# A three-block transformer kernel: the second block's tail in two sections without inner barriers, and the delta scan's output products in another order

## The chip, the cores and the metric

One core of one Trainium2 chip runs the whole program. The metric is the device time of one execution in microseconds (us). Engines are named as in the profile: PE is TensorE's matmul, PEld its weight loads, DVE VectorE, ACT ScalarE, POOL GpSimd, SP SyncE, which issues the DMAs.

## The reference, cut to what matters

Three blocks work on x, 512 tokens of 1024 features, all in float32. What the change touches is the end of the second block, the head of the third, and one recurrence:

```
att_x = blocked_mla(...) @ w_o_mla                      # 8 heads x 128
y_conv = silu(layer_norm(u, ln_g, ln_b)) @ w_pw         # u: depthwise convolution's result
x = x + mx[2] * ((sigmoid(g_conv) * y_conv + sigmoid(g_mla) * att_x) @ w_out)
h = modulate(rms_norm(x, g_ffn), mx[3], mx[4])
a, b = split(h @ w_13);  x = x + mx[5] * ((silu(a) * b) @ w_2)      # hidden width 2816
x = rms_norm(x, g_final)                                # end of the second block
h = layer_norm(x, ln_in_g, ln_in_b)                     # third block
pool_in = h @ w_in[:, :512]                             # then windowed means of pool_in
# gated delta rule, 8 chunks of 64 tokens, 8 heads, state 128 x 128 per head:
v_new = u_n - w_n @ state
o     = qg_n @ state + attn_n @ v_new
state = state * exp(gl_n) + kg_n.T @ v_new
```

## The kernel before, in words

**Layout.** Activations lie feature-major: x is 8 tiles of 128 features by 512 tokens. Every weight matrix comes as a stream of chunks of 512 KB, each 8 tiles of 128 x 128. SP loads chunks into a ring of three (`raw`, `load_chunk` L138). ACT rounds a chunk to the float32r part `whi` (`make_hi`, L144), DVE subtracts to get the rest `wlo` (`make_lo`, L149); both rings have three slots. An activation is split in the same way into `hi` and `lo`, and a product is three matmuls: hi by wlo, lo by whi, hi by whi (L233 to L235 in `linear`, L171 to L173 in `products`). A chunk is therefore 24 matmuls of 128 x 512. A slot is refilled only when the PE is done with its chunk: `next_hi` (L159) waits for `chunk_done`, `next_lo` (L164) follows it, `next_load` (L153) follows that.

**Stages.** `stage` (L73) opens a block of engine programs that ends with a barrier of all engines and a clearing of semaphores. `dense` (L239) is one stage: eight or more output tiles over the stream, evacuated from four PSUM banks. `split_tiles` (L466) is a stage that makes hi and lo of eight tiles. `norm` (L349) is a stage too: with `center` first the sum over features as a product with a matrix of ones (L367), the mean (L378), the subtraction (L399); then squares (L384) and their sum (L371), the factor as Ln and Exp (L386, L388), the scaling (L417), the shift (L421) and, where the output is split, L391 and L406. In the second block after the attention come, each as a stage or two of this kind: split of the attention's output and `dense` by w_o; `norm` of the convolution's result, SiLU with a reload of x, split and `dense` by w_pw; split and `dense` by w_out, which adds into x (L2387); `ffn` (L482): `norm`, `swiglu` (L429, 44 chunks), `dense` over 22 tiles in 24 chunks, `added` (L2396); `norm` by g_final. `third_block` (L2971) goes on with `norm`, and `pool_branch` (L2464) with a memset stage, `dense` of four chunks (L343), the window sums (L2490 to L2500), a split and the product by pool_w.

**The other style.** `macro` (L90) is a block as well, but several matrix products follow in it one after another: each engine has one hand-written program with its own waits. The first block, `conv_and_gates` (L1828) and the attention are written so. `Feed`, `Factor`, `Copies` and `Shift` are pieces of such programs: a `lead` runs two chunks tile by tile, as the activation's tiles come.

**The delta scan** (`delta_scan`, L2751) runs 8 steps. Per step PE makes the state's products (L2779), the solve (L2785), the state's update (L2791) and then, for each of 8 heads, one product with the state's 128 x 128 weights (L2798) and one with 64 x 128 weights (L2799) that adds to the same 64 columns. Each of them is a plain float32 matmul, which the profile shows as two passes. Between the groups lie slices of a background product (three and two per step, three matmuls each). L2835 adds to the state on DVE, L2812 decays it on POOL, L2844 copies the output on ACT.

Of the kernel before, what the change touches and what calls it, by code (L numbers as in the profile page):

```python
# [6 lines left out]
F32 = mybir.dt.float32  # L7
F32R = mybir.dt.float32r
# [538 lines left out]
class Factor:  # L547


    def __init__(self, k, m, x, sq, tmp, rs, bank):  # L550
        self.k, self.x, self.sq, self.tmp, self.rs, self.bank = k, x, sq, tmp, rs, bank
# [8 lines left out]
    act_factor, pe_square = Feed.act_factor, Feed.pe_square  # L560


class Copies:
# [1772 lines left out]
def second_block(k, x, rs, modx, modc, gains, ctx_d, rope_d):  # L2336
# [25 lines left out]
    with nc.sbuf_tensor("gates_place", [P, 72 * 256 + 64], F32):  # L2362
        with nc.sbuf_tensor("o_hi", [P, DT, SEQ], F32R) as oh, \
                nc.sbuf_tensor("o_lo", [P, DT, SEQ], F32R) as ol:
            split_tiles(k, qn, (oh, ol), 8)
            dense(k, DT, DT, (oh, ol), nothing, scaled_by(k, gates[:, 8:16, :], gates[:, 8:16, :]))
        with nc.sbuf_tensor("conv_hi", [P, DT, SEQ], F32R) as uh, \
                nc.sbuf_tensor("conv_lo", [P, DT, SEQ], F32R) as ul:
            mid = u[:, :, HALO:HALO + SEQ]
            norm(k, mid, DT, SEQ, D, 1e-6, lambda t: col(k, "ln_g", t), mid,  # L2370
                 shift=lambda t: col(k, "ln_b", t), center=True)
            with stage(nc, "silu_ready", "landed_x") as (block, silu_ready, landed):
                @block.sync
                def _(sp):
                    sp.dma_start(x[:, :, :], x_saved).then_inc(landed, 16)
                    sp.wait_ge(landed, 16)

                @block.scalar
                def _(act):
                    act.activation(mid, mid, ACT.Silu).then_inc(silu_ready, 1)  # L2380
            split_tiles(k, mid, (uh, ul), 8)
            dense(k, DT, DT, (uh, ul), nothing,
                  scaled_by(k, gates[:, 0:8, :], gates[:, 0:8, :], gates[:, 8:16, :]), ("scaled",))
            split_tiles(k, gates, (uh, ul), 8)

            def add_gated(dve, f, half, bank, S):
                dve.scalar_tensor_tensor(tile_at(x, f), k.ps[:, bank, :], modx[:, bass.ds(f + 16, 1)],  # L2387
                                         tile_at(x, f), ALU.mult, ALU.add).then_inc(S.acc_free, 1)
            dense(k, DT, DT, (uh, ul), nothing, add_gated)

    def add_ffn(y):
        with stage(nc, "added") as (block, added):
            @block.vector
            def _(dve):
                for t in range(DT):
                    dve.scalar_tensor_tensor(x[:, t, :], y[:, t, :], modx[:, 40 + t:41 + t], x[:, t, :],  # L2396
                                             ALU.mult, ALU.add).then_inc(added, 1)
    ffn(k, x, lambda h: norm(k, x, DT, SEQ, D, 1e-6, gf, h, shift=lambda t: modx[:, 24 + t:25 + t]),
        add_ffn)
    norm(k, x, DT, SEQ, D, 1e-6, lambda t: col(k, "g_final", t), x)  # L2400

def norm_tiles(k, tiles, gain, scale, eps, ones="ones", bg=Idle(), slices=0, place=None):
# [55 lines left out]
                    bg.dve(dve, gaps[n // 4])  # L2461


def pool_branch(k, h, mix):  # L2464

    nc = k.nc
    pad = 16
    with ExitStack() as ctx:
        sb = lambda n, s, d=F32: ctx.enter_context(nc.sbuf_tensor(k.name(n), s, d))
        u = sb("pool_in", [P, 4, pad + SEQ])  # L2470
        s = sb("pool_sum", [P, 2, pad + SEQ])
        d = sb("pool_diff", [P, 4, SEQ])
        dh, dl = sb("pool_hi", [P, 4, SEQ], F32R), sb("pool_lo", [P, 4, SEQ], F32R)
        with stage(nc, "zeroed") as (block, zeroed):
            @block.gpsimd
            def _(gp):
                gp.memset(u[:, :, 0:pad], 0.0).then_inc(zeroed, 1)
                gp.memset(s[:, :, 0:pad], 0.0).then_inc(zeroed, 1)
        dense(k, 4, DT, h, copy_out(k, u[:, :, pad:]), nothing)
# [271 lines left out]
def delta_scan(k, q, key, k_tok, v_tok, xt, attn, beta, egc, egl, out, bg, slices):  # L2751
# [3 lines left out]
    with ExitStack() as ctx:  # L2755
# [15 lines left out]
        @block.tensor  # L2771
        def _(pe):
            pe.wait_ge(zeroed, 1)
            for j in range(8):
                tp, T, tk, S = rows(j), j // 2, slice(64 * j, 64 * j + 64), s2[:, j % 2, :, :]
                if j:
                    pe.wait_ge(s_ready, j)
                for h in range(8):
                    mm = pe.matmul(k.ps[tp, h // 4, (h % 4) * P:(h % 4 + 1) * P], key[:, h, tk], S[:, h, :],  # L2779
                                   start=True, stop=True)  # L2780
                mm.then_inc(ks_ready, 1)
                bg.pe(pe, gaps[3 * j])
                pe.wait_ge(r0_ready, j + 1)
                for h in range(8):
                    mm = pe.matmul(k.ps[tp, h // 4, (h % 4) * P:(h % 4 + 1) * P], xt[tp, h, T, :],  # L2785
                                   r0[tp, h, :], start=True, stop=True)
                mm.then_inc(u_done, 1)
                bg.pe(pe, gaps[3 * j + 1])
                pe.wait_ge(vn_ready, j + 1)
                for h in range(8):  # L2790
                    mm = pe.matmul(k.ps[:, 2 + h // 4, (h % 4) * P:(h % 4 + 1) * P],  # L2791
                                   k_tok[tp, T, h * P:(h + 1) * P], vn[tp, h, :], start=True, stop=True)
                mm.then_inc(s_done, 1)
                if j >= 2:
                    pe.wait_ge(o_kept, j - 1)
                for h in range(8):
# [171 lines left out]
        dense(k, n, DT, h, act_evac, dve_evac, ("relu_ready", "sq_ready", "hi_done"))  # L2968


def third_block(k, x, p_d):  # L2971
    nc = k.nc
    gain = lambda name: (lambda t: col(k, name, t))
    with ExitStack() as outer:
        h = tuple(outer.enter_context(nc.sbuf_tensor(n, [P, DT, SEQ], F32R)) for n in ("h3_hi", "h3_lo"))
        norm(k, x, DT, SEQ, D, 1e-5, gain("ln_in_g"), h, shift=gain("ln_in_b"), center=True)
        pool_branch(k, h, x)
# [51 lines left out]
def bass_three_blocks(nc, wstream, vecs, mats, x_t, lora, g_up, c_rows, wmod, ctx_t, rope_t, p_t, out):  # L3029
# [8 lines left out]
    with ExitStack() as ctx:  # L3038
# [18 lines left out]
        second_block(k, x, rs, modx, modc, gains, ctx_t, rope_t)  # L3057
        third_block(k, x, p_t)
        with stage(nc, "stored") as (block, stored):
            @block.sync  # L3060
            def _(sp):
# [193 lines left out]
```

## Time and profile before

| | |
|---|---|
| median of 3 runs | 3924.54 us (3923.83 to 3925.13) |
| profiled execution | 3924.69 us, its span 3922.9 us |
| busy share: PE, DVE, ACT, POOL | 88 %, 45 %, 30 %, 4 % |
| mean granted TensorE clock | 0.912 of full |
| DMA queues' packets | 22.1 % of 16 engines' span |

The span is the time from the first to the last instruction. A group's mean is the duration of one instruction; matmuls overlap, so a matmul's pace is the distance of two starts, which is shorter than its duration. The granted clock is 1.0 at 2.4 GHz and 0.5 at 1.2 GHz.

### The profile page before, as it was taken

What the parts mean: (1) busy time and instruction counts of PE and PEld (TensorE: products, weight loads), DVE (VectorE), ACT (ScalarE), POOL (GpSimd) and SP (SyncE); (2) the same over time, 40 slices, a digit from 0 to 9 for tenths busy, and PEclk for the clock granted to TensorE, in tenths of its full rate; (3) what the DMA queues carried; (4) which work ended last, traced back from release to release, by engine and by line L of the source; (5) the groups of instructions that cost most, each with busy time, mean ns of one, the idle gap of its engine ahead of it and who ended that gap; (6) DMA issues with size and microseconds to landing.
All of it is one profiled execution on the core that took longest, in us unless ns stands there. A gap on an engine that the chain in (4) does not pass through costs nothing. (4 is left out here: it accounts for less than half of the span.)

```text
span 3922.9 us, 43448 instructions
## 1 busy us (share of the span) xinstructions
PE 3434.3 (88%) x17830; PEld 2637.6 (67%) x17830; DVE 1772.0 (45%) x2698; ACT 1191.8 (30%) x1714; POOL 145.0 (4%) x174
## 2 busy tenths in 40 slices
PE   8999988987999999999867999769877896799986
PEld 6887766774688778744555887447656684577764
DVE  4447555533544568577343332335523333433323
ACT  3333332215333333333222222323352202231322
POOL 0000001110000000000000000000014300000000
PEclk9999996788999999989988999879979976899998
DMA  3335210001233633200121222112200000122222
GB/s 130 97 126 207 84 58 8 2 7 57 78 97 122 210 105 98 77 22 0 44 75 59 95 94 93 58 43 89 99 12 23 23 17 32 49 86 89 89 82 74
DMA packets 75221, 285.25 MB, mean 73 GB/s; under 512 B 8336, under 2 KB 8464, under 8 KB 73872
## 3 DMA queue, kind: packets, MB, share of 16 engines
q1 hardware_dynamic: 75024, 282.47, 22.1%
q8 instruction: 142, 2.33, 0.2%
q14 instruction: 55, 0.45, 0.0%
HBM read 276.15 MB, written 6.29 MB: 72 GB/s over the span
## 5 line engine op out<-in xcount | busy, mean ns | idle before, releaser
L149 DVE TENSOR_TENSOR wlo<-raw,whi 128x1024 fp32r<-128x1024 f32 x450 | 552.2, 1227 | 1367.6 <-ACT whi L144 1367.4
L144 ACT ACTIVATE whi<-raw 128x1024 fp32r<-128x1024 f32 x450 | 476.3, 1059 | 1440.4 <-PE ps L235 869.2
L233 PE MATMUL ps<-h_hi,wlo 128*128 128x512 f32 x968 | 389.3, 402 | 94.5 <-DVEq L204 94.5
L234 PE MATMUL ps<-h_lo,whi 128*128 128x512 f32 x968 | 387.6, 400 | 0.0
L235 PE MATMUL ps<-h_hi,whi 128*128 128x512 f32 x968 | 387.1, 400 | 0.0
L171 PE MATMUL ps<-h_hi,wlo 128*128 128x512 f32 x832 | 341.3, 410 | 40.8 <-PEq L80 21.2
L172 PE MATMUL ps<-h_lo,whi 128*128 128x512 f32 x832 | 328.4, 395 | 0.0
L173 PE MATMUL ps<-h_hi,whi 128*128 128x512 f32 x832 | 328.2, 394 | 0.0
L233 PEld LDWEIGHTS ps<-h_hi,wlo 128*128 128x128 f32 x968 | 185.1, 191 | 144.4 <-issue 99.0
L171 PEld LDWEIGHTS ps<-h_hi,wlo 128*128 128x128 f32 x832 | 158.4, 190 | 88.6 <-issue 41.0
L235 PEld LDWEIGHTS ps<-h_hi,whi 128*128 128x128 f32 x968 | 185.0, 191 | 45.7
L234 PEld LDWEIGHTS ps<-h_lo,whi 128*128 128x128 f32 x968 | 185.3, 191 | 45.2
L233 PE MATMUL ps<-mid_hi,wlo 128*128 128x512 f32 x432 | 173.3, 401 | 12.5 <-DVEq L204 12.5
L173 PEld LDWEIGHTS ps<-h_hi,whi 128*128 128x128 f32 x832 | 158.7, 191 | 34.6
L172 PEld LDWEIGHTS ps<-h_lo,whi 128*128 128x128 f32 x832 | 159.1, 191 | 31.9 <-issue 2.2
L1787 DVE SCALAR_TENSOR_TENSOR conv_acc<-u,vecs,conv_acc 128x512 f32<-128x512 f32 x232 | 173.9, 750 | 5.8
L234 PE MATMUL ps<-mid_lo,whi 128*128 128x512 f32 x432 | 172.6, 400 | 0.0
L235 PE MATMUL ps<-mid_hi,whi 128*128 128x512 f32 x432 | 172.6, 400 | 0.0
L173 PE MATMUL ps<-mid_hi,whi 128*128 128x512 f32 x352 | 136.9, 389 | 0.0
L171 PE MATMUL ps<-mid_hi,wlo 128*128 128x512 f32 x352 | 136.9, 389 | 0.0
L172 PE MATMUL ps<-mid_lo,whi 128*128 128x512 f32 x352 | 136.9, 389 | 0.0
L171 PE MATMUL ps<-hx_hi,wlo 128*128 128x512 f32 x304 | 121.9, 401 | 11.1 <-PEq L104 6.5
(545 smaller groups left out, 5846.8 us busy)
## 6 DMA issues: line engine op xcount, KB each, us to landing
raw<-in_wstream SPq DMA_DIRECT2D x453, 512.0 KB, 3.5
mod_ring<-in_wmod SPq DMA_DIRECT2D x48, 512.0 KB, 4.5
c_rows<-in_c_rows SPq DMA_DIRECT2D x3, 1024.0 KB, 5.6
x<-in_x_t SPq DMA_DIRECT2D x4, 512.0 KB, 8.6
x_saved<-x SPq DMA_DIRECT2D x1, 2048.0 KB, 8.9
x<-x_saved SPq DMA_DIRECT2D x1, 2048.0 KB, 7.7
mix_saved_d<-x SPq DMA_DIRECT2D x1, 2048.0 KB, 8.6
mix_back<-mix_saved_d SPq DMA_DIRECT2D x1, 2048.0 KB, 7.8
```

The lines of the kernel that those rows point to most:

```text
L144: act.activation(k.whi[:, n % SPLIT, :], k.raw[:, n % RAW, :], ACT.Copy).then_inc(k.hi_ready, 1)
L149: dve.tensor_tensor(k.wlo[:, n % SPLIT, :], k.raw[:, n % RAW, :], k.whi[:, n % SPLIT, :].bitcast(F32), ALU.subtract).then_inc(k.split_read ...
L171: pe.matmul(out, wlo, hi, start=first, stop=False)
L172: pe.matmul(out, whi, lo, start=False, stop=False)
L173: return pe.matmul(out, whi, hi, start=False, stop=last)
L233: pe.matmul(out, lo, xhi, start=first, stop=False)
L234: pe.matmul(out, hi, xlo, start=False, stop=False)
L235: mm = pe.matmul(out, hi, xhi, start=False, stop=last)
L1787: dve.scalar_tensor_tensor(out, row[:, tap:tap + SEQ], w, acc[:, :], ALU.mult, ALU.add)\
```

## The change

1. From the attention's end to the third block's pooling input there are two `macro` sections: `merge_branches` (24 chunks) and `gated_feed_forward` (44 + 24 + 4 chunks). `pool_branch` keeps its memset stage (now of one tile) and loses its `dense`.
2. In `merge_branches` the convolution's layer norm is done between the chunks of the w_o product, its first sum as seven additions on DVE and one product. In `gated_feed_forward` the silu product's high part is copied by ACT instead of cast by DVE (L449); squares for the two factors go between the chunks; normed values go straight to hi and lo (`Shift`), without L421.
3. `delta_scan` issues the eight products with the state, then the eight with v_new.

The diff, cut; "..." stands for what is left out.

```diff
+def merge_branches(k, x, u, gates, modx, rs, x_saved):
...
+        def _(sp):
+            for i in range(24):
+                next_load(k, sp, g0 + i)
+                if i == 0:
+                    sp.wait_ge(copies.lo, DT)
+                    sp.dma_start(x[:, :, :], x_saved).then_inc(x_in, 16)
...
+            lead(0, copies.lo, oh)
+            for i in range(2, 8):
+                chunk(i, oh)
+                if i == 2:
+                    pe.wait_ge(summed, DT - 1)
+                    pe.matmul(k.ps[:, 4, :], mat(k, "ones"), total[:, :], start=True, stop=True).then_inc(mean_done, 1)
+                if i in (3, 4):
+                    for t in range(4 * (i - 3), 4 * (i - 2)):
+                        conv_square(t)
+            lead(8, lo, ch)
+            for i in range(10, 16):
+                chunk(i, ch)
+            lead(16, g_lo, gh)
+            for i in range(18, 24):
+                chunk(i, gh)
+                factor.pe_square(pe, i - 18)
+            factor.pe_square(pe, 6)
+            factor.pe_square(pe, 7)
...
+            for i in range(24):
+                next_hi(k, act, g0 + i)
...
+                if i == 4:
+                    act.preload_act_table_set("natural_log_exp_and_others")
...
+                    act.preload_act_table_set("silu_and_others")
+                if i in (4, 5):
+                    for t in range(4 * (i - 4), 4 * (i - 3)):
+                        conv_tile(t)      # Silu into mid[t], then Copy into ch[0]
...
+            factor.act_factor(act)
+            act.preload_act_table_set("silu_and_others")
...
+def gated_feed_forward(k, x, modx, gain, rs, pool_in):
...
+            lead(g0, feed)
+            for i in range(2, 2 * FFT):
...
+            for f in range(DT):
+                for c in range(3):
...
+                    if f == 0:
+                        pe.wait_ge(mid_lo, kts[-1] + 1)
...
+                if f:
+                    factor.pe_square(pe, f - 1)
+            factor.pe_square(pe, DT - 1)
+            for t in range(DT):
+                pe.wait_ge(normed, t + 1)
+                mm = pe.matmul(k.ps[:, 6, :], mat(k, "ones"), x[:, t, :], start=t == 0, stop=t == DT - 1)
+            mm.then_inc(mean_done, 1)
+            for t in range(DT):
+                factor3.pe_square(pe, t)
+            lead(gp0, feed3)
+            for i in range(2, 4):
...
@@ delta_scan
                 for h in range(8):
-                    o = k.ps[:, 4 + j % 2, h * 64:h * 64 + 64]
-                    pe.matmul(o, S[:, h, :], q[:, h, tk], start=True, stop=False)
-                    mm = pe.matmul(o, vn[tp, h, :], attn[tp, h, T, :], start=False, stop=True)
+                    pe.matmul(o(h), S[:, h, :], q[:, h, tk], start=h == 0, stop=False, skip_group_check=True)
+                for h in range(8):
+                    mm = pe.matmul(o(h), vn[tp, h, :], attn[tp, h, T, :], start=False, stop=h == 7,
+                                   skip_group_check=True)
```

## Rows read from the trace of the kernel before

**Rows 1.** Stretches from the attention's last matmul to pool_w's first: us, then busy us (count)

```profile
core 0: us, PE busy (x) PEld busy (x) DVE busy (x) ACT busy (x) POOL busy (x), PEclk, DMA share, GB/s
1884.40:1891.40 7.00, 0.05 (x2) 0.07 (x1) 4.90 (x8) 4.87 (x9) 0.00 (x0) 0.77 0.01 1
1891.40:1938.10 46.70, 46.68 (x192) 37.04 (x192) 12.76 (x14) 7.41 (x7) 0.00 (x0) 0.96 0.26 79
1938.10:1983.50 45.40, 14.63 (x32) 5.42 (x33) 20.91 (x34) 17.17 (x22) 0.00 (x0) 0.78 0.16 58
...
2030.20:2040.20 10.00, 0.04 (x1) 0.00 (x0) 7.42 (x11) 5.32 (x9) 0.00 (x0) 0.74 0.18 52
...
2087.60:2120.20 32.60, 9.81 (x16) 3.48 (x17) 16.59 (x26) 14.90 (x21) 0.00 (x0) 0.69 0.05 16
2120.20:2368.50 248.30, 248.26 (x1056) 198.60 (x1056) 88.78 (x106) 57.62 (x66) 0.00 (x0) 0.99 0.29 91
...
2373.10:2498.00 124.90, 124.86 (x528) 100.29 (x528) 28.19 (x23) 27.84 (x30) 0.00 (x0) 0.99 0.30 95
2498.00:2564.30 66.30, 26.60 (x49) 9.71 (x49) 31.61 (x49) 24.88 (x35) 0.21 (x2) 0.72 0.04 15
...
2588.40:2606.70 18.30, 0.00 (x1) 0.00 (x1) 14.39 (x27) 3.73 (x6) 0.00 (x0) 0.58 0.09 30
sum 722.30, PE 589.00 PEld 448.41 DVE 262.96 ACT 184.28 POOL 0.21; mean PE 45.31 PEld 34.49 DVE 20.23 ACT 14.18 POOL 0.02
```

**Rows 2.** Waits of PE in 1884 to 2607: us, times, longest

```profile
PE ps L233 <- DVEq L204: 103.9, 7, 25.5
```

**Rows 3.** Groups of instructions in 1884 to 2607

```profile
L149 DVE TENSOR_TENSOR wlo<-raw,whi 128x1024 fp32r<-128x1024 f32 x96 | 117.7, 1226 | 380.8 <-ACT whi L144 380.8
L144 ACT ACTIVATE whi<-raw 128x1024 fp32r<-128x1024 f32 x96 | 101.7, 1060 | 438.0 <-PE ps L235 438.0
L384 ACT ACTIVATE sq<-x 128x512 f32<-128x512 f32 x24 | 14.9, 628 | 21.2 <-PE ps L371 11.0 <-PEq L80 9.5 <-DVE x L399 0.8
L2387 DVE SCALAR_TENSOR_TENSOR x<-ps,modx,x 128x512 f32<-128x512 f32 x8 | 6.0, 745 | 0.0
L399 DVE TENSOR_TENSOR u<-u,rstd 128x512 f32<-128x512 f32 x8 | 4.9, 684 | 8.1 <-ACT rstd L378 8.1
L388 ACT ACT_TABLE_LOAD x3 | 3.8, 1283 | 0.1
```

**Rows 4.** A stretch at full clock, and the eight steps of the delta scan

```profile
2140.00:2340.00 200.00, 200.00 (x859) 160.29 (x858) 75.04 (x90) 45.78 (x53) 0.00 (x0) 1.00 0.29 95
3120.70:3281.40 160.70, 158.49 (x760) 130.58 (x760) 48.21 (x42) 11.91 (x17) 15.18 (x8) 0.75 0.06 19
```

**Rows 5.** Timeline: sums of squares in the norm before pooling

```profile
2537.18 7.52 PE L371 MATMUL ps<-sq,mats 128*128 128x512 f32 x16 [2.08 <-ACT sq L384]
```

**Rows 6.** Timeline: how `conv_and_gates`, written as a macro section, begins

```profile
1386.43 0.63 ACT L519 ACTIVATE rs<-acc 128x512 f32<-128x512 f32 x1
...
1387.38 1.41 DVE L1811 SCALAR_TENSOR_TENSOR val<-x,mod_gains,rs 128x512 f32<-128x512 f32 x2 [3.37 <-PEq L104]
...
1390.27 0.76 PE L171 MATMUL ps<-hx_hi,wlo 128*128 128x512 f32 x1 [4.60 <-DVE hx_lo L1820]
```

**Rows 7.** Timeline: the third step of the delta scan, update, outputs, next step's first products

```profile
3171.36 2.05 PE L2791 MATMUL ps<-r,k_tok 64*128 64x128 f32 x16
3173.34 0.43 PE L2798 MATMUL ps<-qkv,state 128*128 128x64 f32 x2
...
3173.71 0.43 PE L2799 MATMUL ps<-attn,r 64*128 64x64 f32 x2
...
3181.36 0.69 PE L2799 MATMUL ps<-attn,r 64*128 64x64 f32 x2
3181.97 3.57 PE L2779 MATMUL ps<-state,qkv 128*64 128x128 f32 x16
```

**Rows 8.** Timeline: products of one kind in a row, in the first block's scan and in `delta_matrices`

```profile
861.73 1.10 PE L1410 MATMUL ps<-rw,state 128*128 128x64 f32 x8
...
2919.14 1.95 PE L2710 MATMUL ps<-qkv 128*128 128x128 f32 x16
```

More of the change, by code:

```diff
@@ L547, with __init__ @@
 class Factor:
-    def __init__(self, k, m, x, sq, tmp, rs, bank):
-        self.k, self.x, self.sq, self.tmp, self.rs, self.bank = k, x, sq, tmp, rs, bank
+    def __init__(self, k, m, x, sq, tmp, rs, bank, eps=1e-6):
+        self.k, self.x, self.sq, self.tmp, self.rs, self.bank, self.eps = k, x, sq, tmp, rs, bank, eps
         self.sq_ready, self.sq_used = m.sem("factor_sq_ready"), m.sem("factor_sq_used")
@@ L558, in act_tile, with act_factor @@
         act.activation(self.sq[:, t % 2, :], self.x[:, t, :], ACT.Square).then_inc(self.sq_ready, 1)
-    act_factor, pe_square = Feed.act_factor, Feed.pe_square
+    def act_factor(self, act):
+        act.wait_ge(self.sq_used, DT)
+        act.activation(self.tmp, self.k.ps[:, self.bank, :], ACT.Ln, bias=self.k.eps[self.eps], scale=1.0 / D)\
+           .then_inc(self.logged, 1)
+        act.wait_ge(self.logged, 1)
+        act.activation(self.rs, self.tmp, ACT.Exp, scale=-0.5).then_inc(self.rs_ready, 1)
+    pe_square = Feed.pe_square
 class Copies:
@@ L2360, in second_block @@
         mla_attention(k, qn, qr, kn, kr, vt, scratch, at(k, "mla_stats", 140, [P, 2, 8]), u, acc)
[L2362 to L2394, printed above, removed]
-                for t in range(DT):
[L2396 to L2400, printed above, removed]
+    factor_rs = at(k, "ffn_factor", 136, [P, SEQ])
@@ L2461, in _, with pool_branch @@
                     bg.dve(dve, gaps[n // 4])
-def pool_branch(k, h, mix):
+def pool_branch(k, h, mix, u):
     nc = k.nc
@@ L2469, in pool_branch @@
         sb = lambda n, s, d=F32: ctx.enter_context(nc.sbuf_tensor(k.name(n), s, d))
-        u = sb("pool_in", [P, 4, pad + SEQ])
         s = sb("pool_sum", [P, 2, pad + SEQ])
@@ L2476, in _ @@
             def _(gp):
-                gp.memset(u[:, :, 0:pad], 0.0).then_inc(zeroed, 1)
                 gp.memset(s[:, :, 0:pad], 0.0).then_inc(zeroed, 1)
-        dense(k, 4, DT, h, copy_out(k, u[:, :, pad:]), nothing)
         with stage(nc, "step", "hi_ready", "lo_ready") as (block, step, hi_ready, lo_ready):
@@ L2795, in _ @@
                     pe.wait_ge(o_kept, j - 1)
+                o = lambda h: k.ps[:, 4 + j % 2, h * 64:h * 64 + 64]
                 for h in range(8):
-                    o = k.ps[:, 4 + j % 2, h * 64:h * 64 + 64]
-                    pe.matmul(o, S[:, h, :], q[:, h, tk], start=True, stop=False)
-                    mm = pe.matmul(o, vn[tp, h, :], attn[tp, h, T, :], start=False, stop=True)
+                    pe.matmul(o(h), S[:, h, :], q[:, h, tk], start=h == 0, stop=False, skip_group_check=True)
+                for h in range(8):
+                    mm = pe.matmul(o(h), vn[tp, h, :], attn[tp, h, T, :], start=False, stop=h == 7,
+                                   skip_group_check=True)
                 mm.then_inc(o_done, 1)
@@ L2968, in relu_square, with third_block @@
         dense(k, n, DT, h, act_evac, dve_evac, ("relu_ready", "sq_ready", "hi_done"))
-def third_block(k, x, p_d):
+def third_block(k, x, h, pool_in, p_d):
     nc = k.nc
@@ L2974, in third_block @@
     with ExitStack() as outer:
-        h = tuple(outer.enter_context(nc.sbuf_tensor(n, [P, DT, SEQ], F32R)) for n in ("h3_hi", "h3_lo"))
-        norm(k, x, DT, SEQ, D, 1e-5, gain("ln_in_g"), h, shift=gain("ln_in_b"), center=True)
-        pool_branch(k, h, x)
+        outer.enter_context(nc.sbuf_tensor("h3_place", [P, 32 * 256 + 64], F32))
+        with nc.sbuf_tensor("pool_place", [P, 9 * 256], F32):
+            pool_branch(k, h, x, pool_in)
         with nc.sbuf_tensor("qkv3", [P, 24, SEQ], F32) as qkv:
@@ L3056, in bass_three_blocks @@
         rs, modx, modc, gains = first_block(k, x, vecs, mats, x_t, lora, g_up)
-        second_block(k, x, rs, modx, modc, gains, ctx_t, rope_t)
-        third_block(k, x, p_t)
+        h, pool_in = second_block(k, x, rs, modx, modc, gains, ctx_t, rope_t)
+        third_block(k, x, h, pool_in, p_t)
         with stage(nc, "stored") as (block, stored):
```

279 lines of the change are left out of this document (added).

## The prediction

> **What bounds the kernel now.** I read the busy shares first: PE at 88 % of the span, so time is PE's work, its pace, and its gaps. Then I cut the changed stretch, from the attention's last matmul to the first product by pool_w, into its stages [rows 1]. It lasts 722.3 us with PE busy for 589.0. The stages are of two kinds. In the dense ones PE never stops: 192 matmuls take 46.7 us, the 44 chunks of the gated product 248.3. Between them PE idles or does a few sums: 7.0, 45.4, 10.0, 32.6, 66.3 and 18.3 us, and 4.6 more between 2368.5 and 2373.1. The waits of PE say the same: 103.9 us in seven waits at the start of a dense stage [rows 2], where PE stands at a barrier while DVE and ACT prepare a whole activation. The pace at full clock is 200/859 = 0.233 us a matmul [rows 4], 5.6 us a chunk; a dense stage of eight chunks should take 44.8 and takes 46.7, since its first matmuls run at 1.2 GHz (clock 0.96) after the gap. So each gap costs itself and about 1.9 us.
>
> ACT and DVE have room: in the gated product DVE is busy 88.8 of 248.3 us, ACT 57.6, DMA 29 % [rows 1].
>
> The delta scan is another picture: 160.7 us for eight steps, PE busy nearly throughout, granted clock 0.75 [rows 4]. Of a step of 20.1 us the output products take 3181.97 - 3173.34 = 8.63 us for 32 passes [rows 7].
>
> **The change, part by part.** Sections first, as seen by PE.
>
> *Opening.* Eight tiles are split before a barrier now: 7.0 us [rows 1]. With a lead, one tile suffices: seven ACT copies of 0.62 (one pass, as L384 [rows 3]) and the closing barrier (some 0.4) go, 2.3 us are left.
>
> *First section, stream.* 24 chunks are 134.4 us; one ramp stays, 1.8: 136.2. Added among them are single float32 sums. Eight of them took 7.52 us [rows 5], 0.94 each with some waiting; I take 0.9 in a stream. The section has 17 (1 for the mean, 8 convolution squares, 8 of x), down from 24 in the two norms; 14 lie between chunks: 12.6 us.
>
> *First section, the one new wait.* The convolution's SiLU and copies stand on ACT behind the refills of chunks 7 and 8, four tiles each time. A tile costs ACT two passes, 2 x 0.63, and DVE 0.75 + 0.69 [rows 3], in a chain of about 1.4 us. I followed the queues: chunk 4 ends, ACT refills (1.06), loads a table (1.28), waits for the last square, takes Ln and Exp and a second table load, then four tiles, 5.6 us. By then chunk 5 is over; refill 8, four more tiles, and only then refill 9, whose DVE half (1.23) ends about 3 us after chunk 7. The lead of w_pw needs chunk 9, so PE waits **3.1 us**, between 0 (if DVE and ACT overlap better) and 12 (if the two chains run one after another). Squares and subtractions before it are ready when PE comes to them.
>
> *The other two leads.* At chunk 15's end ACT and DVE need 1.06 + 1.23 + 3 x 0.69 + 0.62 = about 5 us for the last merged tile, but the lead uses that tile 9.8 us later: no gap, where 10.0 us and a ramp were.
>
> *First section's tail.* After chunk 23: refill 2.3, the sum into x 0.75, square 0.63, waits: 4.0; last sum 0.9; Ln and Exp 1.4; table load 1.28; barrier 0.3; then values, high and low part of the first tile. The existing section gives 1390.27 - 1387.38 = 2.9 us for the last step, with a table load of ACT in it [rows 6]; here it lies ahead of the barrier, so 2.3. Sum 10.2.
>
> First section: 2.3 + 136.2 + 12.6 + 3.1 + 10.2 = 164.4, against 7.0 + 46.7 + 45.4 + 46.7 + 10.0 + 47.4 + 32.6 = 235.8 us (the two dense stages not shown are of the pattern of the first). **Saved 71.4.**
>
> *Second section.* The gated product keeps 248.3; its lead is paced by DVE (2 x 0.75 a tile against PE's 1.4), +0.3. The cast leaves DVE for ACT, both under cover: per two chunks ACT has 2 x 1.06 + 2 x 0.62 = 3.4 us in 11.2. The 4.6 us gap goes. The product over 22 tiles is 22 x 5.6 = 123.2, plus six sums of 0.9: 128.6 (124.9 before, with a ramp). Then the two norms, 66.3 us now. After: last tile's sum to factor 6.3, eight scalings 6.0 with the feature sums behind them (PE lags at the low clock, +2.7), mean 0.7, subtraction and first square 1.4, eight sums 7.5 [rows 5], factor 1.5, first tile of the lead 2.4: 28.5. The two sums are chained by data, so the change can't remove them; four table loads of 1.28, three barriers, L2396's 6 us and seven tiles of splitting go. Pool's four chunks: 24.3 (24.1 before). After them 18.3 us, now with one more stage in the way (the memset): +1.3. Sum 248.6 + 128.6 + 28.5 + 24.3 + 19.6 = 449.6 against 486.5. **Saved 36.9.**
>
> Costed at nothing: x's reload (2 MB) now stands in SP's queue between weight loads. A ring of three raw chunks covers 16.8 us, and DMA is at 30 % at most [rows 1]; without that cover the next refill would be late by the reload's time. POOL's memset in the second section is waited for by nobody but the end. Together **108.3**, bounds 98 (the wait at 12, one more ramp) and 118 (no wait, no lag).
>
> *Delta scan.* Alternating, two passes are 0.37 us apart at full clock and 0.61 at the low one (3173.71 - 3173.34, 3181.97 - 3181.36) [rows 7]. Products of one kind in a row: eight passes of exactly this shape, 128 x 128 weights and 64 columns, in 1.10 us including the last one's run-out, and 16 with 128 columns in 1.95 [rows 8]: 0.115 a pass. Low clock: 3.57/16 = 0.22 (L2779) [rows 7]. The clock falls inside the group, where PE streams little: 10 passes at 0.185 and 22 at 0.305 make the 8.6 us, so some 2 us in. Over the scan it is at the low level half of the time (0.75). Three outcomes per step:
> - clock stays up: outputs 32 x 0.115 = 3.7, next products 1.9 instead of 3.57, the rest 7.9: 13.5, saving 6.6, **52** in all;
> - clock drops 2 us in as now: 17 passes done by then, 15 more at 0.22, next products at 3.57: 5.3 + 3.57 + 7.9 = 16.8, saving 3.3, **27**;
> - pace is not set by the alternation: **0**.
>
> Grouped passes still stream 64 columns per load of 128, so PE stays half empty there; I take the middle. DVE's addition to the state, 1.2 us for 1024 columns as L149's [rows 3], is ready before the outputs' 3.7 us are over, and POOL's decay (15.18/8 = 1.9 us [rows 4]) is wanted only after the next update; neither becomes late.
>
> Here the row and a rule differ. Rows 8 show weights of the same shape loading beside the running matmul: 16 passes at 0.12 us, where a load of 128 x 128 alone is busy for 37.04/192 = 0.19 [rows 1]. The Trainium skill (TensorE: Matmul & The Clock Gate, "The mechanism") says that weight loads overlap with running matmuls only when the row group differs; with that, grouping like with like gains nothing. The trace speaks against it, and it is the third outcome above. The same page ("What's actually happening") holds that activity releases the throttle; the first outcome would be that rule at work.
>
> **Sum.** The profiled execution is 3924.7 us (span 3922.9 and 1.8 around it), 0.1 above the median. 3924.7 - 108.3 - 27 = **3789**.
>
> **Rivals.**
> - *Clock stays up in the scan.* For: denser passes. Against: they are still half empty. 3924.7 - 108.3 - 52 = 3764.
> - *The order in the scan buys nothing.* Against it rows 8, for it that only the alternating pair was ever seen with accumulation. 3816.
> - *The first section stalls.* The layer norm's chain is 12 us late and later gaps pull the clock down, also in the second section's tail: some 20 us back, 3809.
> - *Slower than before.* The mechanism: in a barrier-free section refills stand behind other work on ACT's and DVE's queues; once the way from a chunk's end to its slot's refill (2.3 us bare) exceeds the two chunks in hand, 11.2 us, PE waits at every chunk. To lose 8 us net each of the 96 chunks would have to wait (135 + 8)/96 = 1.5 us. Against it: DVE's busiest chunk in the steady part has 3.3 us, only chunks 4 and 5 have more. 3933.
>
> **How the numbers follow.** Forecast 0.59, clock up 0.15, order nothing 0.12, first section stalls 0.11, slower 0.03. The range takes the forecast with its bounds and most of the next two: 3760 to 3816. Within 0.2 % (8 us, what a measurement can tell) lies almost nothing: 0.01; faster 0.96.
>
> **What would show it.** Right: no wait of PE over 4 us between attention and pooling except before the second section (10 us) and in the two norms (28); one of about 3 at w_pw's lead; the stretch to pool_w's first product 614 us long; in the scan 5.3 us from the first output product to the next step's first, steps of 16.8. Wrong: output passes further apart than 0.13 us at full clock, a granted clock in the scan still at 0.75, or PE waiting for `wlo` inside a chunk stream.

## The result, and the profile of the changed kernel

The changed kernel takes **3747.36 us** (median of 4 runs, 3744.08 to 3754.97) against 3924.18 (4 runs beside it, 3919.36 to 3925.13): ratio 0.9554, 95 % interval 0.9541 to 0.9568. I had forecast 3789, and 3760 to 3816 as the range. The sign was right, the size was 42 us short. The profiled execution is 3744.08 us, its span 3742.1.

The stretches of the changed kernel, to be laid beside [rows 1] and [rows 4]; columns as there:

```profile
1876.38:1929.56 53.18, 53.18 (x210) 40.48 (x210) 34.24 (x49) 27.78 (x40) 0.00 (x0) 0.97 0.27 99
...
1932.65:2036.11 103.46, 96.02 (x401) 76.05 (x401) 44.68 (x55) 31.78 (x38) 0.00 (x0) 0.96 0.29 92
2036.11:2402.00 365.89, 365.89 (x1592) 300.73 (x1593) 122.34 (x131) 105.60 (x125) 0.00 (x0) 0.99 0.31 95
2402.00:2436.44 34.44, 23.41 (x43) 8.78 (x41) 14.50 (x22) 11.31 (x17) 0.15 (x1) 0.80 0.10 31
2436.44:2460.09 23.65, 23.64 (x96) 19.05 (x96) 12.23 (x16) 8.87 (x12) 0.00 (x0) 0.93 0.22 67
...
2990.75:3105.10 114.35, 111.61 (x760) 96.36 (x760) 48.30 (x42) 11.90 (x17) 15.18 (x8) 0.97 0.08 27
2100.00:2280.00 180.00, 180.00 (x796) 149.07 (x795) 60.69 (x67) 53.30 (x66) 0.00 (x0) 1.00 0.32 97
```

The first section (1873.96 to 2036.11, with the two waits of 2.4 and 3.1 us that the next view shows) takes 162.2 us, the second with the stage behind it 443.0. Together 605.1, against 722.3 before. The waits of PE in this stretch (us in all, times, longest). Before, the seven waits at the start of a dense stage took 103.9 us [rows 2], and those in the norms 29.5 more:

```profile
PE ps L233 <- DVEq L204: 19.0, 1, 19.0
PE ps L171 <- DVE h_lo L1827: 9.3, 2, 5.4
PE ps L528 <- ACT sq L558: 4.9, 2, 2.9
PE ps L171 <- DVE wlo L149: 3.1, 1, 3.1
PE ps L171 <- DVE o_lo L582: 2.4, 1, 2.4
PE ps L2632 <- DVE x L2713: 2.2, 1, 2.2
PE ps L528 <- ACT conv_sq L558: 2.0, 1, 2.0
```

Of the seven waits at the start of a dense stage one is left, the 19.0 us ahead of pool_w. A step of the scan, which answers to [rows 7]:

```profile
3028.57 2.05 PE L3114 MATMUL ps<-r,k_tok 64*128 64x128 f32 x16
3030.55 2.00 PE L3123 MATMUL ps<-qkv,state 128*128 128x64 f32 x16
3032.48 2.00 PE L3125 MATMUL ps<-attn,r 64*128 64x64 f32 x16
...
3034.40 1.96 PE L3102 MATMUL ps<-state,qkv 128*64 128x128 f32 x16
```

From the first output product to the next step's first product are 3.85 us; before 8.63. The scan takes 114.35 us instead of 160.7, at a granted clock of 0.97 instead of 0.75.

**Where the 180.8 us of the two profiled spans come from**, read off the times of the same landmarks in both:

| part | before | after | difference | forecast |
|---|---|---|---|---|
| up to the attention's end (code unchanged) | 1884.4 | 1874.0 | -10.4 | 0 |
| attention's end to pool_w's first product | 722.3 | 605.1 | -117.2 | -108.3 |
| from there to the scan | 514.0 | 511.7 | -2.3 | 0 |
| delta scan | 160.7 | 114.35 | -46.4 | -27 |
| after the scan | 641.5 | 636.9 | -4.6 | 0 |

The first row is not the change's. In both kernels the same program runs there, and its time differs from one execution to the next: it has more than one course. The changed kernel from 590 to 640 us, columns as above (the granted clock stands third from the end), first in the profiled execution, then in a later one of the same kernel (a13 below):

```profile
590.00:640.00 50.00, 41.22 (x618) 33.41 (x618) 30.61 (x116) 16.18 (x53) 9.91 (x14) 0.89 0.01 2
```

```profile
590.00:640.00 50.00, 44.18 (x392) 35.39 (x392) 22.35 (x94) 12.57 (x42) 8.49 (x12) 0.62 0.03 12
```

At 0.62 the attention ends at 1885.6, as in the kernel before (1884.4). Of the 18 traces of this study two end it by 1875.4, two between 1878.7 and 1880, thirteen between 1883 and 1886, and one (a3), whose first block has its operands moved, at 1914. What tips it I did not find. The totals below carry this difference, so runs are compared by stage. Ten of the fifteen variants were timed once; their totals rest on one execution each.

### The profile page after: what moved, and what is told of

Its sections match the earlier page's. It is cut to its first block and busy times, and to the rows that moved or that the text cites. A ratio compares the mean times of both kernels' runs of the same rounds, so it can differ in the third digit from the quotient of the medians.

```text
span 3742.1 us, 43214 instructions
## 1 busy us (share of the span) xinstructions
PE 3339.5 (89%) x17816; PEld 2592.6 (69%) x17816; DVE 1754.9 (47%) x2659; ACT 1201.4 (32%) x1732; POOL 145.0 (4%) x174
## 3 DMA queue, kind: packets, MB, share of 16 engines
q1 hardware_dynamic: 75024, 282.47, 23.3%
## 5 line engine op out<-in xcount | busy, mean ns | idle before, releaser
L171 PE MATMUL ps<-mid_hi,wlo 128*128 128x512 f32 x528 | 207.8, 394 | 0.0
L173 PE MATMUL ps<-mid_hi,whi 128*128 128x512 f32 x528 | 205.4, 389 | 0.0
L172 PE MATMUL ps<-mid_lo,whi 128*128 128x512 f32 x528 | 205.4, 389 | 0.0
L172 PE MATMUL ps<-hx_lo,whi 128*128 128x512 f32 x304 | 120.0, 395 | 0.0
L173 PE MATMUL ps<-hx_hi,whi 128*128 128x512 f32 x304 | 119.6, 393 | 0.0
L171 PEld LDWEIGHTS ps<-mid_hi,wlo 128*128 128x128 f32 x528 | 99.1, 188 | 21.9 <-issue 1.4
```

Of the source, the lines that this page charges most:

```text
L171: pe.matmul(out, wlo, hi, start=first, stop=False)
L172: pe.matmul(out, whi, lo, start=False, stop=False)
L173: return pe.matmul(out, whi, hi, start=False, stop=last)
```

## Experiments: the delta scan's order

**One part alone, from both sides.** a1 puts the old order into the changed kernel, b1 the new order into the old one.

```diff
+                for h in range(8):
+                    pe.matmul(o, S[:, h, :], q[:, h, tk], start=True, stop=False)
+                    mm = pe.matmul(o, vn[tp, h, :], attn[tp, h, T, :], start=False, stop=True)
```

> The changed kernel with the delta scan's outputs in the old, alternating order. Nothing else is touched. Theory (the scan's 46 us come from the order alone, as pace and as clock): the scan goes from 114 us back to about 160, granted clock in it from 0.97 to about 0.75, the time from 3747 to 3793. Rival (the scan gained because the stages ahead of it now leave the clock in a better state, the order gives only part): the scan stays between 125 and 145 us, time 3760 to 3778.

> The kernel before with the new order in the delta scan and nothing else. Theory (order alone): scan 160.7 to about 114 us, time 3924 - 46 = 3878. My forecast's own case (the clock still drops): 3924 - 27 = 3897, granted clock about 0.85. Rule that like row groups cannot overlap their loads: 3924.

Measured: a1 3803.1 us (ratio to before 0.969, interval 0.9668 to 0.9711; the 10 us over the expected 3793 are the first block's longer course, its attention ends at 1885.1), b1 3880.8 (0.9892, interval 0.9868 to 0.9915). The scans, a1 then b1:

```profile
3004.00:3163.40 159.40, 157.71 (x760) 130.13 (x760) 48.20 (x42) 11.90 (x17) 15.15 (x8) 0.76 0.06 19
```

```profile
3122.50:3238.80 116.30, 113.75 (x760) 98.03 (x760) 48.29 (x42) 11.90 (x17) 15.16 (x8) 0.95 0.08 26
```

The order alone is worth 45.1 and 44.4 us in the scan, whatever stands ahead of it. Both rivals fall, my forecast's 27 among them.

**What in the order costs.** Two things had changed at once: how often the kind of weights changes, and whether a product adds to the 64 columns just written. a4 keeps the first and takes away the second; a5 does the reverse, with the state's product made twice per head, and so leaves out the product of attn and v_new. Both orders in short form:

```diff
# a4                                       # a5
+for h in range(9):                        +for h in range(8):
+    if h < 8: state(h)                    +    state(h)
+    if h: values(h - 1)                   +    state(h)     # adds to the same columns
```

> The changed kernel, outputs in the order state(0), state(1), values(0), state(2), values(1) and so on: kinds alternate, but the two products of one head no longer follow each other on the same 64 columns of PSUM. Theory A (a switch between weights of 128 rows and weights of 64 rows costs): passes 0.185 us apart at full clock, outputs 8.6 us, clock falls as in the kernel before, scan 160 us. Theory B (adding to the columns just written costs): 0.12 us a pass, outputs 3.9 us, scan 114 us.

> The changed kernel; per head the product with the state is made twice, one right behind the other, the second adding to the columns of the first. It leaves out the product of attn and v_new in the outputs. Theory A (switch of shapes costs): no switches, 0.12 us a pass, outputs 3.9 us, scan 114 us. Theory B (adding to columns just written costs): about 0.185 us a pass and 160 us.

Timelines of PE, a4 and then a5:

```profile
3054.77 0.43 PE L3123 MATMUL ps<-attn,r 64*128 64x64 f32 x2
3055.13 0.43 PE L3122 MATMUL ps<-qkv,state 128*128 128x64 f32 x2
3055.49 0.43 PE L3123 MATMUL ps<-attn,r 64*128 64x64 f32 x2
```

```profile
3025.78 3.79 PE L3122 MATMUL ps<-qkv,state 128*128 128x64 f32 x32
3029.49 1.96 PE L3102 MATMUL ps<-state,qkv 128*64 128x128 f32 x16
```

a4: still 0.36 us for a pair of passes, scan 156.8 us, 3799.9 in all. a5: 32 passes in 3.71 us, scan 111.8. So it is the change between products of 128 rows and products of 64, not the accumulation. Weights and moving operand change their rows together; no run parts the two. The traces show where the time goes: in a row of one kind the load of the next weights begins 0.055 us after the start of the pass before it (changed kernel), and at a change 0.20 us after it (a1, at 3037.04 behind 3036.83). The Trainium skill (TensorE: Matmul & The Clock Gate, "The mechanism") has loads overlap with running matmuls only where the row group differs. The traces do not bear that out: in a row of one kind a load onto the same rows begins 0.055 us into a pass that lasts 0.275, and the order in which the rows change is the slower one. a6 halves the number of changes:

```diff
+for h in range(0, 8, 2):
+    state(h); state(h + 1); values(h); values(h + 1)
```

> The changed kernel, outputs in groups of two heads: two state products, two value products, and so on (8 changes of kind per step where the old order has 16 and the new one 2). If each change of kind costs PE 2 x (0.185 - 0.12) = 0.13 us at full clock: 3.9 + 6 x 0.13 = 4.7 us for the outputs as long as the clock holds. If the clock holds the scan is 114 + 8 x 0.8 = 121 us; if it falls as in the old order, outputs 7 and next products 3.5 us, scan about 150.

```profile
3045.86 0.66 PE L3122 MATMUL ps<-qkv,state 128*128 128x64 f32 x4
...
3050.56 3.24 PE L3102 MATMUL ps<-state,qkv 128*64 128x128 f32 x16
```

Outputs 3050.56 - 3045.86 = 4.70 us at full clock, just as priced at 0.13 us a change. The scan takes 143.1 us at a clock of 0.80 (3780.9 in all): between the two, and nearer the slow one. In this step the clock fell 5.2 us behind the first output, when the outputs were over; in the other seven it fell 2.0 to 3.7 us behind it, among them.

**The clock.** At full clock throughout, the alternating outputs would take 32 x 0.1825 = 5.84 us, 2.0 more than the grouped ones. That is 16 us in eight steps; by this estimate the other 30 of the 46 are the clock, which in the old order is low for the later outputs and the next step's products. Two runs ask what holds it up: a7 adds two large products among alternating outputs, a10 makes the grouped outputs twice over.

```diff
# a7, in the old order's loop over h
+    if h in (2, 5):
+        pe.matmul(k.ps[:, 0, :], mat(k, "ident"), q[:, h, :], start=True, stop=True)
# a10
+for again in range(2):
+    for h in range(8): state(h)
+    for h in range(8): values(h)
```

> The changed kernel with the old, alternating order and two extra float32 products of 512 columns per step among the outputs (behind heads 2 and 5, into a bank that is free there, result unused). Theory (the alternation's small products leave PE too idle, so the clock falls, and that is two thirds of the 46 us): with dense work between them the clock stays up; outputs 32 x 0.185 + 2 x 0.9 = 7.7 us, next products 1.95, steps about 17.6, scan some 141 us although work was added. Rival (the clock isn't what slows the outputs): 160 + 8 x 1.8 = 175 us.

> The changed kernel, new order, every step's output products made twice over (8 state, 8 value, and the same again, which writes the same result). Added: 16 products, 32 passes a step. If the density of the passes keeps the clock up: 8 x 3.85 = 31 us more, scan 145 us at a granted clock of 0.97, time 3778. If the length of the stretch of small products decides, whatever their order: the clock falls in the second half, outputs about 10 us and next products 3.5, scan about 114 + 8 x 8 = 178 us, granted clock about 0.8.

```profile
3032.70 0.62 PE L3122 MATMUL ps<-qkv,state 128*128 128x64 f32 x2
3033.25 0.69 PE L3123 MATMUL ps<-attn,r 64*128 64x64 f32 x2
3033.87 2.07 PE L3125 MATMUL ps<-qkv,mats 128*128 128x512 f32 x2
...
3127.57 1.13 PE L3125 MATMUL ps<-qkv,mats 128*128 128x512 f32 x2
```

```profile
3037.05 2.00 PE L3122 MATMUL ps<-qkv,state 128*128 128x64 f32 x16
...
3040.91 2.00 PE L3122 MATMUL ps<-qkv,state 128*128 128x64 f32 x16
3042.84 3.37 PE L3123 MATMUL ps<-attn,r 64*128 64x64 f32 x16
3046.13 3.67 PE L3102 MATMUL ps<-state,qkv 128*64 128x128 f32 x16
...
3123.67 2.38 PE L3123 MATMUL ps<-attn,r 64*128 64x64 f32 x16
```

My theory fell in a7 by its number: 178.3 us for the scan, where the rival had 175 and I 141. In the step shown the clock had fallen before the first added product, and two of them did not bring it back; the first four steps went like it, with the clock falling 1.6 to 2.0 us behind the first output. In the fifth and the seventh it fell 0.2 and 0.4 us after the first added product had begun. In the sixth (3127.57) and the eighth both added products went at full pace (1.13 us for 2.07) and the clock stayed up through the outputs: the sixth step took 19.2 us where the first five took 23.3 to 24.5.

In a10 the scan takes 175.6 us where 178 stood for "the length of the stretch decides", and the clock falls in each of the eight steps, in grouped order too. In the step shown first, passes go at 0.12 us until some 6 us behind the first output. That is the latest of the eight: the others fall 3.4 to 5.9 us behind it, and in two of them within the first sixteen products (3123.67). In the alternating order the clock falls in every step as well, 1.9 to 3.6 us behind the first output (a1; 1.5 to 3.3 in the kernel before). With grouped outputs made once it falls in one of the changed kernel's eight steps, 4.2 us behind the first output and among the next products (L3102 3.41 us at 3048.25), and in one of b1's, 2.9 us behind it; in a5 it falls in none.

So that grouping holds the clock up is shown, from both sides. Why is not shown in full. With the length doubled at the same density it was lost in every step (a10), which speaks for the length; but in two of these steps it fell before the second half began, so what went before in the scan plays a part too. Grouped outputs are also denser than alternating ones, and no run changed the density alone. The time of the fall moves by up to 3 us from step to step within one trace, and that it would fall in only one step of eight could not be worked out from these figures. The Trainium skill (TensorE: Matmul & The Clock Gate, "What's actually happening") says that activity releases the throttle; a7's sixth step agrees, and its first steps show that added activity behind the fall was not enough here.

## Experiments: where the operands lie

In the changed kernel at full clock 796 products go in 180 us, 0.226 each; before, 859 in 200, 0.233 [rows 4]. The difference follows the moving operand. Before, activations of the dense stages start 64 bytes past a multiple of 128 (h3_hi at byte 79168 of its partition in the built program); hand-placed ones start at a multiple (79232). The sections use hand-placed ones, and so does h3, which the third block reads. Four runs move operands and nothing else.

```diff
# b2, a2 (16 floats), b3 (8 floats)      # a3
+        sb("pad", [P, 16])              -        k.arena = PERSISTENT
         k.arena = PERSISTENT            +        k.arena = PERSISTENT - 64
```

> The kernel before with one unused tensor of 64 bytes a partition ahead of the stack's later tensors, so that every activation of the dense stages starts 64 bytes later: at a multiple of 128 bytes, where it was 64 past one. Nothing else changes. Theory (the moving operand's start sets the pace): all 128x512 products of the dense stages go from 0.2333 to 0.2267 us apart, some 5200 of them, 5200 x 0.0066 = 34 us, time 3924 to 3890. Rival (the pace belongs to the style of the stage: loops, semaphores, bank order): no change, 3924.

> The changed kernel with the same 64-byte tensor. Only the third block's o, mid and p operands (about 1010 products) still start 64 past a multiple of 128 in it. Theory (start of the moving operand): 1010 x 0.0066 = 6.7 us, time 3747 to 3741. Rival (style of the stage): 3747.

> The changed kernel with every hand-placed tensor 64 bytes lower, so that the operands of the barrier-free sections of all three blocks start 64 past a multiple of 128 bytes. Theory (the moving operand's start sets the pace): some 9400 products go from 0.2267 to 0.2333 us; where PE sets the pace that is up to 62 us, time some 3747 + 50 to 60 = 3800 to 3809. Rival (style of the stage): 3747.

> The kernel before with the dense stages' operands 32 bytes higher, 96 past a multiple of 128 bytes (before: 64 past; with 64 bytes more, at the multiple: 0.2267 us a product). If only a start at a multiple of 128 is fast: 0.2333 us, time 3924. If the pace grows with what is off a multiple of 64 too: above 0.2333.

200 us at full clock in b2, b3 and a3; the number behind PE's busy time is its count:

```profile
2140.00:2340.00 200.00, 200.00 (x884) 165.62 (x883) 76.27 (x91) 47.66 (x56) 0.00 (x0) 1.00 0.31 97
```

```profile
2140.00:2340.00 200.00, 200.00 (x859) 161.02 (x858) 75.04 (x90) 46.25 (x54) 0.00 (x0) 1.00 0.30 94
```

```profile
2140.00:2340.00 200.00, 200.00 (x859) 160.29 (x858) 64.92 (x71) 58.07 (x71) 0.00 (x0) 1.00 0.29 95
```

With 64 bytes more the old kernel's stages run at 0.226; with 32 they stay at 0.233; the changed kernel, moved off, falls back to 0.233. The style of the stage has no part in it.

The times are smaller than the counts of products gave. b2: 3905.4 us (ratio 0.9952, interval 0.9936 to 0.9969), 19 us where I expected 34. By stage it gains 10.7 us between attention and pool_w and 10.6 behind the scan, and nothing between them, where it is 2.5 longer (as are b1 and b3 by 2.1 and 2.0, without faster products). In the first of these stretches the dense streams gained 15.3 us, as 96 x 24 x 0.0066 = 15.2 says, and the norm behind w_o gave back 4.6, because its sums ran at the low clock. First the kernel before, then b2:

```profile
1941.35 7.11 PE L367 MATMUL ps<-u,mats 128*128 128x512 f32 x16 [3.27 <-PEq L80]
1950.54 7.52 PE L371 MATMUL ps<-sq,mats 128*128 128x512 f32 x16 [2.07 <-ACT sq L384]
```

```profile
1940.83 10.15 PE L367 MATMUL ps<-u,mats 128*128 128x512 f32 x16 [3.27 <-PEq L80]
1953.06 9.09 PE L371 MATMUL ps<-sq,mats 128*128 128x512 f32 x16 [2.08 <-ACT sq L384]
```

Between pool_w and the scan the q, k, v projection ends with DVE's convolution, so a faster pace there only lengthens PE's wait at the stage's end. This wait is 6.95 us in the kernel before (first row) and 10.67 in the changed kernel (second row), and 10.67 in b2 as well:

```profile
2815.17 0.77 PE L233 MATMUL ps<-h_hi,wlo 128*128 128x512 f32 x1 [6.95 <-DVEq L204]
```

```profile
2685.53 0.77 PE L233 MATMUL ps<-h_hi,wlo 128*128 128x512 f32 x1 [10.67 <-DVEq L204]
```

a2: behind the scan 630.3 us for 636.9, 6.6 where 6.7 was expected. Its median is 3747.8 (ratio 0.9553, interval 0.9532 to 0.9574), since its first block took the longer course (attention's end at 1885.9). a3: 3801.1 us; 11.0 more in the changed stretch (616.1 for 605.1; by the count of products 15.2, but its w_o stream ran at a clock of 1.00 for 0.97 and the tail of the norms was 1.1 us shorter), 2.8 between it and the scan, 3.2 behind the scan, and the attention ends 28.5 us later than in a13 (1914.1 for 1885.6). b3: 3925.1, no change.

## Experiments: the sections

**The first section as stages again** (on operands at the new placement, with one stage more for the factor of x):

```diff
-        merge_branches(k, x, u, gates, modx, factor_rs[:, :], x_saved)
+            split_tiles(...); dense(...); norm(...); stage silu, reload of x
+            split_tiles(...); dense(...); split_tiles(...); dense(..., add_gated)
+        factor_stage(k, x, factor_rs[:, :])
```

> The changed kernel with the first section undone: split, dense, norm, silu, split, dense, split, dense as stages with barriers, as before the change, on operands at the new placement, and one more stage for the factor of x. The second section and the scan's order stay. Theory (the first section's gaps are worth what they last): the stretch from the attention to the gated product goes from 162 to about 235.8 - 3.8 (pace) - 16 (half of the old norm moved into the second section's opening) = 216 us, time 3747 + 54 = 3801. Rival (part of the gain is only moved, since the second section's own stretches lengthen with a denser first section): less than 40 us.

```profile
PE ps L233 <- DVEq L204: 42.3, 3, 25.3
```

The stretch takes 663.2 us for 605.1: the first section is worth 58.1 us there, against 54 expected, and the three waits at barriers are back (6.95, 25.3 and 10.0). The sums of the convolution's norm ran at the low clock, as in b2 (10.11 and 9.09 us, against 7.11 and 7.52 in the kernel before); that is 4.6 us, about what the result lies over 54. The two kernels with this norm behind a w_o stage at the faster pace, b2 and a9, both show it, and those at the slower pace do not; the cause is open. 3813.8 us in all: of the 69.7 us over the changed kernel, 58.1 are these, 1.5 lie in the first block, and 10.3 went behind them (5.4 between pool_w and the scan, 2.0 in it, 2.9 after it), where the code is the same; why, no run shows.

**The wait at w_pw's lead.** Rows of the changed kernel at that lead: ACT comes to its refills behind the last convolution tile, DVE to the first of two behind the last low part.

```profile
1929.76 0.63 ACT L2466 ACTIVATE conv_hi<-u 128x512 fp32r<-128x512 f32 x1
1930.30 1.99 ACT L144 ACTIVATE whi<-raw 128x1024 fp32r<-128x1024 f32 x2
1930.43 0.69 DVE L2511 TENSOR_TENSOR conv_lo<-u,conv_hi 128x512 fp32r<-128x512 f32 x1 [0.59 <-ACT conv_hi L2466]
1931.37 1.23 DVE L149 TENSOR_TENSOR wlo<-raw,whi 128x1024 fp32r<-128x1024 f32 x1 [0.25 <-ACT whi L144]
...
1932.65 0.80 PE L171 MATMUL ps<-conv_hi,wlo 128*128 128x512 f32 x1 [3.10 <-DVE wlo L149]
```

a8 spreads the tiles over three chunks:

```diff
-                if i in (4, 5):
-                    for t in range(4 * (i - 4), 4 * (i - 3)):
+                if i in (4, 5, 6):
+                    for t in range((0, 3, 6)[i - 4], (3, 6, 8)[i - 4]):
```

> The changed kernel with the convolution's tiles on ACT and DVE spread over three chunks (3, 3 and 2 tiles behind the refills of chunks 7, 8 and 9) instead of two (4 and 4). Theory (the lead of w_pw waits because the refill of chunk 9 stands behind eight tiles of other work on both queues): the refill comes some 1.4 us earlier on each queue and the wait of 3.1 us at that lead goes to nearly nothing, about 3 us off the stretch. Rival (the chain through the last tiles sets the lead anyway): the wait stays at about 3 us under another name.

```profile
PE ps L171 <- DVE wlo L149: 0.5, 1, 0.5
```

The wait is gone but for 0.5 us, and with it the low clock behind it: 4.0 us off the first section. Another 3.1 us went in the second section's tail, where the clock was low for 10.2 us instead of 17.1, at a point that this edit only moved in time; that part is luck. The stretch is 598.2 us; the whole, 3749.0, has the first block's longer course (attention's end at 1885.8).

**The tail of the norms** took 34.4 us where I had 28.5. In the changed kernel:

```profile
2411.29 10.00 PE L2632 MATMUL ps<-x,mats 128*128 128x512 f32 x16 [2.23 <-DVE x L2713]
2423.37 9.21 PE L528 MATMUL ps<-sq,mats 128*128 128x512 f32 x16 [2.08 <-ACT sq L558]
```

a11 fills PE's waits there:

```diff
+            keep_busy(11)      # float32r products of 512 columns, into a free bank
             factor.pe_square(pe, DT - 1)
+            keep_busy(9)
...
+            keep_busy(8)       # ahead of the eight sums of squares
...
+            keep_busy(14)      # ahead of lead(gp0, feed3)
```

> The changed kernel with unused float32r products of 512 columns in the waits of PE in the two norms behind the second section's product (11, 9, 8 and 14 of them, some 0.23 us each, about as long as the waits of 2.9, 2.2, 2.1 and 3.9 us). Theory (the tail took 34.4 us where I had 28.5 because the clock fell in these waits, which drew the sums from 7.5 to 10.0 and 9.2 us): the clock stays up, both groups of sums at 7.5 us, tail 29 to 31 us, some 4 us off. Rival (the sums are paced by DVE and ACT): no gain, or the products' own delay on top.

```profile
2422.29 7.13 PE L2638 MATMUL ps<-x,mats 128*128 128x512 f32 x16 [0.18 <-DVE x L2721]
2428.86 2.40 PE L2605 MATMUL ps<-mid_lo 128*128 128x512 f32 x8
2431.50 7.70 PE L528 MATMUL ps<-sq,mats 128*128 128x512 f32 x16 [0.24 <-ACT sq L558]
```

The clock stays up, the sums take 7.1 and 7.7 us, the tail 2443.07 - 2413.93 = 29.1. 5.3 us of the term's 5.9 were the clock. Pool's four chunks behind it took 1.6 us less too, at a clock that stayed up. (3749.4 us in all, again with the longer course.)

**All three together, and the changed kernel beside it.**

> The changed kernel with three things together: all operands of the third block at a multiple of 128 bytes (6.6 us in the pair of traces), the convolution's tiles over three chunks (3 us), products in the waits of the norms (4 us). Expected 3 + 4 + 6.6 = 13.6 us under the changed kernel run beside it, 3747 to about 3734; if spreading and busy products give nothing, 3741. The first block's own 11 us (its fast or slow course) may fall either way and is taken out by stage.

> The changed kernel once more, unchanged, on the same chip and beside the last. Expected 3747 (3744 or 3755, by which of two courses the first block takes); from the end of the first block on its trace should agree with the first one within 0.5 us.

a12: **3737.3 us** (3735.5 to 3740.0; ratio 0.9535, interval 0.9515 to 0.9555). a13: 3755.7 (3755.25 to 3762.5; 0.9586, interval 0.9568 to 0.9604). a12 is 18 us under the changed kernel on the same chip, and 10 under the median of its first four runs, so it beats both kernels. By stage, against the first trace: the stretch 594.4 for 605.1, the part behind the scan 630.5 for 636.9. The two edits of the stretch do not add up: each alone gave 6.95 us, together they gave 10.7, since the 3.1 us that a8 gained in the tail are part of what the added products gain there. a13's own profiled execution is 18.4 us longer than the first: 11.7 in the first block, 1.9 in the scan, 4.9 around it. My expectation that it agrees within 0.5 us behind the first block held as far as the scan's approach (2945 us in the first trace) and no further.

## Why the prediction was wrong, step by step

The profiled gain exceeds the forecast's 135.3 us by 45.5: 19.4 in the scan, 10.4 ahead of the change, 8.9 in the two sections, 4.6 behind the scan and 2.3 between pool_w and the scan (each rounded).

- **The scan, sized by the middle outcome.** This is the largest miss: 27 forecast, 46.4 measured. The pace of grouped passes was right (0.12 us from [rows 8]), and the outcome in which grouping gains nothing did not come. The step that failed is "clock drops 2 us in as now": I took the fall and its time from the alternating order [rows 7] and carried them over. In grouped order there was no fall in seven of eight steps, of the changed kernel and of b1 alike, and the changed kernel's one fall came when the outputs were over. The outcome "clock stays up", 52 us at a chance of 0.15, was nearly it: six steps of 13.8 to 14.5 us against 13.5, and two of 15.3 and 15.4, one with that fall and one, the first, that began at the low clock. With the measured 46.4 in place of 27 the forecast would have been 3770.
- **The pace, 5.6 us a chunk.** I carried 0.233 us from the old stages [rows 4] into stages with other operands. Products of the new sections take 0.227. By the count of products that is 15.2 us of the stretch, and a3 measured 11.0; of the 4.6 us behind the scan, 3.2 are of the same kind by a3, through h3. [rows 4] held no hint of the cause, but the starts of the first block's products in the same trace are 0.227 us apart, and I did not ask why.
- **Ahead of the change, 10.4 us** of the profiled difference. Nothing in the change; a forecast made against one execution should carry this as an error of its own. It does not excuse the range: the slowest of the first four runs, 3754.97, lies below 3760 as well.
- **The first section**: 162.2 us for 164.4. Opening 2.4 (2.3 forecast), new wait 3.1 (3.1), no wait at w_out, tail in waits 2.0 and 5.4. Stream and tail together took 53.2 + 103.5 = 156.7 for 159.0; the faster pace alone gives 24 x 24 x 0.0066 = 3.8, so the rest was forecast 1.5 too short. a8 shows the cause of the wait as forecast.
- **The second section**: 443.0 for 449.6. Its stream took 365.9 for 377.2 (pace), its tail 34.4 for 28.5: I had counted 2.7 us for the low clock, in one group of sums; both groups ran partly at it (10.0 and 9.2 us, 7.1 and 7.7 in a11). The gap ahead of pool_w was forecast as 19.6 and took 19.0.
- **The reload of x and the memset, costed at nothing**: no wait of PE names them.
- **Rivals**: no chunk stream waits for `wlo`, so the slower outcome and the stalling section did not come. The range ended 13 us short on the fast side, since "clock up" and the sections' bounds were added but no bound stood for pace.

## What to carry to other kernels

Group small products by the shape of their weights: each change between products of 128 and of 64 rows cost 0.13 us at full clock, and more through the clock, which held in seven steps of eight with grouped outputs (3.85 us) and fell in all eight with alternating ones (5.84 us at full clock) or with grouped ones made twice. Try moving operands at a multiple of 128 bytes of the partition; a 64-byte pad bought 0.5 % of a kernel whose PE is 88 % busy. Count what a faster pace gives only where PE sets the pace, and look at the clock in the stages behind it. Before pricing a rewritten stage by an old stage's pace, look for a stage of the new style in the same trace and explain any difference.

## What the runs showed of the hardware

- A 128x512 float32r product at full clock: 0.227 us with its moving operand at a multiple of 128 bytes, 0.233 at 64 or 96 past it (884 against 859 products in 200 us).
- Two runs of the same program can take courses 11 us apart where engines wait on each other in small steps: granted clock 0.89 or 0.62 in the same 50 us of the first block, and after it the two traces keep their distance within 0.5 us for 1000 us.
- Unused float32r products in waits of 2 to 4 us kept the clock up in the norms (a11); two float32 products set in after the fall did not raise it in the scan (a7, four steps of eight). In two more steps it fell within the first of them, and in two it stayed up.
- At a change between 128-row and 64-row products the next load begins 0.20 us after the start of the pass before it, in a row of one kind 0.055 us (a1 and the changed kernel); a pass then takes 0.1825 us on average for 0.12.
- The same sums in the norm behind w_o took 7.11 and 7.52 us in the kernel before, and 10.1 and 9.1 in b2 and a9, by the clock alone.
